# A 256-token, two-model chain of layers on one core: the RWKV time-mixing layer in another order (r and gate projections ahead of v, scores early, one table set for log and exp, bonus by wide matmuls)

## The reference

```python
def rwkv7_time_mix(h, mu, w_r, w_k, w_v, w_o, w0, w1, w2, a0, a1, a2, g1, g2, k_k, k_a, r_k, ln_g, ln_b):
    xx = jnp.pad(h, ((0, 0), (1, 0), (0, 0)))[:, :-1] - h
    xr, xw, xk, xv, xa, xg = [h + xx * mu[i] for i in range(6)]
    r, k, v = xr @ w_r, xk @ w_k, xv @ w_v
    w = -jax.nn.softplus(-(w0 + jnp.tanh(xw @ w1) @ w2)) - 0.5
    a = jax.nn.sigmoid(a0 + (xa @ a1) @ a2)
    g = jax.nn.sigmoid(xg @ g1) @ g2
    kk = heads(k * k_k); kk = kk / norm(kk)          # 16 heads of 64
    k = k * (1 + (a - 1) * k_a)
    decay = jnp.exp(-jnp.exp(heads(w)))
    # per token: S = S*decay + (S @ -kk) (kk*a)^T + v k^T ; y = S @ r
    y = group_norm(y) * ln_g + ln_b
    bonus = jnp.sum(r * k * r_k, -1, keepdims=True) * v
    return ((y + bonus) * g) @ w_o
```

## Time and profile before

| | us |
|---|---|
| median of 3 runs | 2113.77 (2110.63 to 2114.1) |
| the profiled execution's own time | 2107.99 |
| its span, from the first to the last instruction | 2106.2 |
| PE busy in it | 1939.2 |
| of it, the time-mixing layer up to its output projection | about 1115 to 1384 |

### The profile page before, as it was taken

The page is one execution under the profiler, slowest core; times in us unless marked ns, Lnnn a source line. Parts: engine busy times, 40 slices in busy tenths (PEclk is TensorE's granted clock), DMA queues, the critical chain, the costliest instruction groups (busy, mean ns, idle before and its releaser), DMA issues.

```text
span 2106.2 us, 21632 instructions
## 1 busy us (share of the span) xinstructions
PE 1939.2 (92%) x8583; PEld 1426.7 (68%) x8583; DVE 556.3 (26%) x1339; ACT 416.1 (20%) x989; POOL 56.4 (3%) x68
## 2 busy tenths in 40 slices
PE   6999899787689999999998889989999899999998
PEld 4777678666546777677776677847777667737774
DVE  1000202453311000200005853430000343623344
ACT  1000200132111000200006720340000234312431
POOL 0200000000000000000000303000000000000000
PEclk9999999755589999999999985699999999999999
DMA  5745534200033444445453230023545675366630
GB/s 201 246 151 178 124 120 120 100 1 1 0 98 122 137 162 148 133 138 173 127 168 96 95 106 21 1 80 102 178 132 144 112 115 97 74 105 82 101 101 20
DMA packets 190869, 232.21 MB, mean 110 GB/s; under 512 B 22868, under 2 KB 172696, under 8 KB 190792
## 3 DMA queue, kind: packets, MB, share of 16 engines
q1 hardware_dynamic: 188032, 223.85, 38.9%
q0 software_dynamic: 1840, 5.12, 0.8%
q10 hardware_dynamic: 920, 2.16, 0.3%
HBM read 230.07 MB, written 1.05 MB: 110 GB/s over the span
## 4 chain that ended last, share of the span: by engine, by line
PE 63%; DVE 4%; PEld 2%; issue 2%; ACT 2%; POOL 0%; PEldq 0%; DVEq 0%
PE ps L501 22%; PE ps L274 14%; PE ps L519 10%; PE ps L458 5%; PEld ps L274 2%; PE ps L1548 1%; PE ps L1399 1%; PE ps L542 1%; PE ps L2022 1%; PE ps L2038 1%; PE ps L2026 1%; PE ps L1565 1%; PE ps L357 1%; PE ps L2052 1%; PE ps L2057 1%
## 5 line engine op out<-in xcount | busy, mean ns | idle before, releaser
L501 PE MATMUL ps<-hT,ring 128*128 128x256 f32 x2816 | 624.0, 380 | 0.7 <-issue 0.7
L501 PEld LDWEIGHTS ps<-hT,ring 128*128 128x128 f32 x2816 | 536.8, 191 | 108.3 <-issue 39.3
L274 PE MATMUL ps<-hT,ring 128*128 128x272 f32 (+3 forms) x1408 | 334.6, 392 | 5.5 <-issue 3.0
L274 PEld LDWEIGHTS ps<-hT,ring 128*128 128x128 f32 (+2 forms) x1408 | 256.0, 185 | 67.0 <-issue 11.7
L519 PE MATMUL ps<-ring,arena 128*128 128x512 f32 x640 | 287.7, 592 | 0.0
L573 DVE TENSOR_TENSOR arena<-arena,ps 128x256 f32<-128x256 f32 x88 | 37.1, 421 | 850.5 <-ACT arena L558 850.5
L519 PEld LDWEIGHTS ps<-ring,arena 128*128 128x128 f32 x640 | 121.6, 190 | 118.9 <-issue 114.8
L558 ACT ACTIVATE arena<-ps 128x256 f32<-128x256 f32 x88 | 33.8, 384 | 845.0 <-PE ps L501 845.0
L274 PE MATMUL ps<-arena 128*128 128x64 f32 (+6 forms) x384 | 104.3, 439 | 16.5 <-DVE arena L1261 12.7
L458 PE MATMUL ps<-ring,arena 128*128 128x512 f32 (+1 forms) x256 | 112.6, 596 | 1.5 <-ACT arena L2087 0.8
L274 PEld LDWEIGHTS ps<-arena 128*128 128x128 f32 (+2 forms) x384 | 83.9, 309 | 33.0 <-DVE arena L1261 14.8
(11 more groups left out here) (355 smaller groups left out, 1645.6 us busy)
## 6 DMA issues: line engine op xcount, KB each, us to landing
ring<-in_ffn_w_gate SPq DMA_DIRECT2D x44, 1024.0 KB, 5.3
ring<-in_ffn_w_up SPq DMA_DIRECT2D x44, 1024.0 KB, 5.4
ring<-in_ffn_w_down SPq DMA_DIRECT2D x44, 1024.0 KB, 5.0
ring<-in_w_in SPq DMA_DIRECT2D x32, 1024.0 KB, 10.7
ring<-in_ab_w_in SPq DMA_DIRECT2D x13, 1024.0 KB, 5.4
ring<-in_w_out SPq DMA_DIRECT2D x8, 1024.0 KB, 5.0
ring<-in_ab_w_out SPq DMA_DIRECT2D x6, 1024.0 KB, 5.1
ring<-in_c_w_k SPq DMA_DIRECT2D x4, 1024.0 KB, 5.6
```

The costliest lines, as they stand in the source:

```text
L274: last = nc.tensor.matmul(o, l, r, start=(i == 0), stop=(i == len(pairs) - 1))
L501: m = nc.tensor.matmul(ps[:, 4 + j % 2, 256 * w:256 * (w + 1)], slot8(s0 + 3 * q + w)[:, k, c * P:(c + 1) * P], hT[:, k, META:], start=(k ...
```

## The change

All of it is in the time-mixing layer and in the order of its weights.

1. TensorE's list: r blocks 0 and 1 go ahead of `sig`; `pair_scores(0)` comes after r 3, (1) after r 5, (2) and (3) after g1, which now comes before v. The last score bank goes to VectorE, which copies its diagonal blocks and, after the solve, the rest of it.
2. The bonus is 8 matmuls of 256 columns with 16-column weights (`rsel`), a copy to SBUF by VectorE (`bsum`) and two small transposes, all between `tok` and m32.
3. m32 waits for the first two copies of VectorE's t64 scatter alone; the scatter of `tts` is waited for behind m32 and the first g2 piece. Two g2 pieces stand behind t64 instead of one before it.
4. ScalarE loads the table set that has both Ln and Exp by name, and the Tanh/Sigmoid set once; `key_root(7)` comes before Tanh. It makes 1 + (a - 1)*k_a (Identity with scale and bias) where VectorE had a tensor_scalar. The copy of g1's output comes before `decays(7)`, its Sigmoid before v's evictions.
5. VectorE scans into a buffer of its own (`csum`), so that `mid` is no step of the chain, and has one instruction less per block.

The diff, cut to its core:

```diff
+            r_part = square("c_w_r")
+            plan.append(r_part[0])
                          ((64, P), 0, (1, D), d["c_a2"][0].rearrange("p (o n) -> p o n", o=1))])
-            plan += square("c_w_r") + square("c_w_v")
+            plan += r_part[1:]
             plan.append([(P, 0, (KD, 160), d["c_g1"][0].rearrange("(k p) n -> p k n", p=P))])
+            plan += square("c_w_v")
...
-                n = [turn_a("x", p2, 0), turn_a("x", p2, 1)]
+                o = [bank_a(turn_a("x", p2, 0)), bank_d(turn_d("x", p2, 1)) if p2 == 3 else bank_a(turn_a("x", p2, 1))]
...
-                                m.then_inc(to_act, 1)
+                                m.then_inc(to_dve if p2 == 3 and hh == 1 else to_act, 1)
...
             norm_product(KD - 1)
+            pe.wait_ge(mix_ready, 4 * KD)
...
+            def r_product(j):
+                w = r_slot[j // 2]
...
+                n = turn_a("r", j)
+                m = group(bank_a(n)[:, 0:S], [(slot8(w)[:, c, (j % 2) * P:(j % 2 + 1) * P], MB[3][:, c, :]) for c in range(KD)])
+                m.then_inc(to_act, 1)
...
+            r_product(0)
+            r_product(1)
+            s += 1
             take_slot(pe, s)
...
                     nc.tensor.matmul(bank_a(n[i])[:, 0:S], ring[64 * i:64 * i + 64, s % NSLOT, j * P:(j + 1) * P],
                                      low[64 * i:64 * i + 64, :], start=True, stop=True).then_inc(to_act, 1)
             pe.drain().then_inc(slot_used, 1)
+            s += 4
+            r_product(2)
+            r_product(3)
+            pair_scores(0)
+            r_product(4)
+            r_product(5)
+            pair_scores(1)
+            r_product(6)
+            r_product(7)
+            take_slot(pe, s)
+            pe.wait_ge(mix_ready, 6 * KD)
+            g1 = ring[:, s % NSLOT, 0:KD * 160].rearrange("p (k n) -> p k n", k=KD)
+            n = turn_a("g1")
+            group(bank_a(n)[:, 0:S], [(g1[:, c, 0:P], MB[5][:, c, :]) for c in range(KD)])
+            group(bank_a(n)[0:32, S:2 * S], [(g1[:, c, P:160], MB[5][:, c, :]) for c in range(KD)]).then_inc(to_act, 1)
+            pe.drain().then_inc(slot_used, 1)
+            pe.drain().then_inc(mix_used, 1)
             s += 1
-            pe.wait_ge(mix_ready, 4 * KD)
-            for j in range(KD):
-                if j % 2 == 0:
-                    take_slot(pe, s)
-                n = turn_a("r", j)
-                group(bank_a(n)[:, 0:S], [(slot8(s)[:, c, (j % 2) * P:(j % 2 + 1) * P], MB[3][:, c, :]) for c in range(KD)])\
-                    .then_inc(to_act, 1)
-                if j % 2 == 1:
-                    pe.drain().then_inc(slot_used, 1)
-                    s += 1
-                if j >= 4:
-                    pair_scores(j - 4)
-            pe.wait_ge(mix_ready, 5 * KD)
+            pair_scores(2)
+            pair_scores(3)
...
-            n = turn_d("bonus")
-            for t in range(T):
-                for k in range(KD):
-                    m = group(bank_d(n)[:, t * 16 + 2 * k:t * 16 + 2 * k + 2], [(w_rk[:, k, t * P:(t + 1) * P], rsel[:, k, :])])
-            m.then_inc(to_dve, 1)
-            take_slot(pe, s)
-            pe.wait_ge(mix_ready, 6 * KD)
-            g1 = ring[:, s % NSLOT, 0:KD * 160].rearrange("p (k n) -> p k n", k=KD)
-            n = turn_a("g1")
-            group(bank_a(n)[:, 0:S], [(g1[:, c, 0:P], MB[5][:, c, :]) for c in range(KD)])
-            group(bank_a(n)[0:32, S:2 * S], [(g1[:, c, P:160], MB[5][:, c, :]) for c in range(KD)]).then_inc(to_act, 1)
-            pe.drain().then_inc(slot_used, 1)
-            pe.drain().then_inc(mix_used, 1)
-            s += 1
+            n = turn_d("bonus", 0)
+            group(bank_d(n)[64:80, 0:S], [(rsel[:, 16 * k:16 * k + 16], w_rk[:, k, :]) for k in range(KD)]).then_inc(to_dve, 1)
...
-                pe.wait_ge(act_out, job["g1",])
+                pe.wait_ge(act_out, job["v", 0])
...
-            pe.wait_ge(sc_dve, 2)
-            pe.wait_ge(sc_act, 1)
+            pe.wait_ge(dve_out, job["bonus", 0])
+            n = turn_d("bonus", 1)
+            for t in range(T):
+                m = nc.tensor.transpose(bank_d(n)[:, 16 * t:16 * t + 16], bsum[:, t * P:(t + 1) * P], ident[64:80, 64:80])
+            m.then_inc(to_dve, 1)
+            pe.wait_ge(sc_dve, 1)
...
             g2_product(0, 0)
+            pe.wait_ge(sc_dve, 2)
+            pe.wait_ge(sc_act, 1)
...
-            g2_product(1, 0)
...
+            g2_product(1, 0)
             g2_product(1, 1)
...
+                for hh in range(1 if p2 == 3 else 2):
+                    diag, left, corner = score_parts(next_a(), p2, hh)
...
+            nc.scalar.preload_act_table_set(LN_EXP)
...
-            nc.scalar.activation(low[0:64, :], b[0:64, 0:S], ACT.Tanh)
-            nc.scalar.activation(low[64:P, :], b[64:P, 0:S], ACT.Copy).then_inc(act_out, 1)
-            for j in range(KD):
-                nc.scalar.activation(w_ep[:, j, :], next_a()[:, 0:S], ACT.Sigmoid, bias=colB[:, 48 + j:49 + j]).then_inc(act_out, 1)
-                nc.scalar.activation(w_a[:, j, :], next_a()[:, 0:S], ACT.Sigmoid, bias=colB[:, 56 + j:57 + j]).then_inc(act_out, 1)
+            nc.scalar.activation(low[64:P, :], b[64:P, 0:S], ACT.Copy)
             key_root(7)
-            for j in range(KD):
+            nc.scalar.preload_act_table_set("sigmoid_and_others")
+            nc.scalar.activation(low[0:64, :], b[0:64, 0:S], ACT.Tanh).then_inc(act_out, 1)
+            def r_out(j):
+                nc.scalar.activation(w_r[:, j, :], next_a()[:, 0:S], ACT.Copy).then_inc(act_out, 1)
...
-                nc.scalar.activation(w_r[:, j, :], next_a()[:, 0:S], ACT.Copy).then_inc(act_out, 1)
-                if j >= 4:
-                    scores_out(j - 4)
...
+            r_out(0)
+            r_out(1)
+            act.wait_ge(kfix_in, 1)
+            for j in range(KD):
+                nc.scalar.activation(w_ep[:, j, :], next_a()[:, 0:S], ACT.Sigmoid, bias=colB[:, 48 + j:49 + j]).then_inc(act_out, 1)
+                alink(act, nc.scalar.activation(w_a[:, j, :], next_a()[:, 0:S], ACT.Sigmoid, bias=colB[:, 56 + j:57 + j]))
+                nc.scalar.activation(MB[2][:, j, :], w_a[:, j, :], ACT.Identity, scale=colB[:, 72 + j:73 + j],
+                                     bias=kfix[:, j:j + 1]).then_inc(act_out, 1)
+            nc.scalar.preload_act_table_set(LN_EXP)
+            decays(0)
+            r_out(2)
+            decays(1)
+            r_out(3)
+            decays(2)
+            scores_out(0)
+            r_out(4)
+            decays(3)
+            r_out(5)
+            decays(4)
+            scores_out(1)
+            r_out(6)
+            decays(5)
+            r_out(7)
+            decays(6)
+            b = next_a()
+            nc.scalar.activation(sg1, b[:, 0:S], ACT.Copy)
+            nc.scalar.activation(sg2, b[0:32, S:2 * S], ACT.Copy).then_inc(act_out, 1)
+            decays(7)
+            scores_out(2)
+            scores_out(3)
             alink(act, nc.scalar.activation(emid, mid[:, :, 1], ACT.Exp, scale=-DECAY))
             nc.scalar.activation(eend, w_c[:, :, P - 1], ACT.Copy).then_inc(emid_done, 1)
+            alink(act, nc.scalar.activation(sg1, sg1, ACT.Sigmoid))
+            alink(act, nc.scalar.activation(sg2, sg2, ACT.Sigmoid))
...
-            b = next_a()
+            nc.scalar.preload_act_table_set(LN_EXP)
             act.wait_ge(solved, 1)
-            nc.scalar.activation(sg1, b[:, 0:S], ACT.Sigmoid)
-            nc.scalar.activation(sg2, b[0:32, S:2 * S], ACT.Sigmoid).then_inc(act_out, 1)
-            act.wait_ge(tt_zero, 3)
+            act.wait_ge(tt_zero, 2)
...
-            for k in range(KD):
-                nc.vector.tensor_scalar(rsel[:, k, :], const("pairsel"), col(80, k), None, ALU.mult)
+            nc.vector.tensor_scalar(kfix, colB[:, 72:80], -1.0, 1.0, ALU.mult, ALU.add).then_inc(kfix_in, 1)
...
+            dve.wait_ge(mix_ready, 6 * KD)
+            dlink(dve, nc.vector.memset(rsel, 0.0))
+            for a in range(2):
+                nc.vector.tensor_scalar(rsel[:, a:a + 127 - 1 + 1:18], colB[:, 80:88], const("pairsel")[:, a:a + 1], None, ALU.mult)
...
-                        m = nc.vector.tensor_tensor_scan(w_c[:, j, tk], ones, w_ep[:, j, tk], 0.0, ALU.mult, ALU.add)
+                        m = nc.vector.tensor_tensor_scan(csum[:, t, :], ones, w_ep[:, j, tk], 0.0, ALU.mult, ALU.add)
                     dlink(dve, m)
                     c2 = w_c[:, j, :].rearrange("p (t n) -> p t n", t=T)
-                    dlink(dve, nc.vector.tensor_copy(mid[:, j, :], c2[:, :, 63]))
-                    dlink(dve, nc.vector.tensor_tensor(c2, c2, mid[:, j, :].rearrange("p (t o) -> p t o", o=1).broadcast_to([P, T, P]),
-                                                       ALU.subtract))
+                    dlink(dve, nc.vector.tensor_tensor(c2, csum, csum[:, :, 63:64].broadcast_to([P, T, P]), ALU.subtract))
+                    nc.vector.tensor_copy(mid[:, j, :], csum[:, :, 63])
```

(23 more changed lines are left out.)

44 lines of the change are left out of this document (29 added, 15 removed).

## The result

The changed kernel takes 2080.24 us (median of 4 runs, 2079.41 to 2081.34) against 2112.54 for the kernel before: a ratio of 0.9848, 95% interval 0.9834 to 0.9863, or 32 us less. Forecast were 2099.8, with a range of 2086 to 2110. The sign was right and the time outside the range: the gain is more than twice the forecast's.

The account below looks back on a forecast made before the run. Three limits in turn: VectorE's per-block chain, the chain from solve to m32, then TensorE at half clock. -12.1 and -2.8, with 1 back for the clock, gave -14: 2099.8 us from a 2113.77 median, range 2086 to 2110.

Parts of the forecast that it names:

- The start of the chain: Start of VectorE's per-block chain: `sig` 2.6 us later, 1.25 us a block on ScalarE, first block ready 2.4 us later.
- TensorE between `sig` and the solve: TensorE has more to do than the wait allows, with `decays(7)` behind g1's evictions; the solve starts 2.8 us later.
- From the solve to m32: After the solve, v, `tok`, wide bonus (3.5 us) and VectorE's copies let m32 start at 1250.0, 12.1 us earlier.
- m32 to the end of chunk t = 0: Same matmuls in another order, 37.50 and 50.07 us at clock 0.50; no change taken.
- Chunk t = 1: Group norm in the last chunk: fewer table loads, so roots are waited for less, 2.8 us saved (1.3 to 4.4).
- The clock stays at 1.00 through m32 to chunk t = 0: Rival: TensorE keeps full clock from m32 through chunk t = 0, another 28 us off, 2072 us; chance 0.10.
- The slower rival: Rival: the clock is not back in time, chunk t = 1 takes 50.07 us instead of 34.24; 2118.6 us, chance 0.05.
- The gain is eaten before the solve: Rival: clock falls and queued evictions between first scores and solve start the solve 10 us later; 2110 us, chance 0.07.

Follow-up runs that it names:

- e15_k_on_vector: e13_high_last with the key's factor computed on VectorE again and without ScalarE's Identity: 2077.10 us.
- e14_bonus_narrow: e13_high_last with the wide bonus undone: 128 matmuls of 2 columns again, no copy and no transposes of the sum: 2077.23 us.
- e5_delay_17: The changed kernel with one extra matmul of 432 columns in front of g2(1,1), to hold TensorE up by 1.7 us: 2106.31 us.
- e3_tables_own: The changed kernel without the four lines that name a table set, so the compiler picks the sets (34 loads in the layer): 2107.96 us.
- e13_high_last: The changed kernel with the last g2 matmuls reordered, the two over 32 rows ahead of the two over 128 rows: 2096.89 us.
- e12_version2: e4 with ScalarE's `tts[1]` scatter earlier, g2's 32-row halves spread and all four 128-row halves ahead of chunk t = 0: four runs 2065.46 to 2072.91 us, one 2095.18.
- e1_g2_apart: The changed kernel with g2(1,0) put back between the m64 and t64 products: 2080.07 us.
- e9: e3_tables_own with the last two g2 pieces reordered, both 32-row matmuls first, then both 128-row ones: 2081.66 us.
- e17: e13_high_last with one extra matmul of 256 columns ahead of its last g2 pieces, to hold TensorE up by 1.0 us: 2081.00 us.
- e2: The kernel before with only g2(1,0) moved from between m64 and t64 to right ahead of g2(1,1): 2095.99 us.
- e6: The kernel before with extra matmuls of 512 and 80 columns in front of g2(1,1), to hold TensorE up by 2.3 us: 2090.22 us.
- e4: The changed kernel with the wide bonus ahead of `tok`, t64 copies ahead of the bonus sum's, m32 ahead of the bonus transposes: 2077.25 us.
- e7: e3_tables_own with one extra matmul of 256 columns in front of g2(1,1), to hold TensorE up by 1.0 us: 2083.51 us.
- e8: The kernel before with only the change's table sets named: five runs at 2082.86 to 2091.22 us, five at 2107.28 to 2109.78.

## Why the prediction was wrong

*The start of the chain, +2.4; measured +4.05.* `sig` was right (+2.5 for +2.6). The block was not: from the first block's first Sigmoid to the second's it is 1.38 us (1174.52 to 1175.90), for the 1.25 taken, and all eight take 11.25 for 10.0. The mis-sized term is the Identity: 0.60 us long, and 0.51 from its start to the next Sigmoid's, for 0.40. e15_k_on_vector takes it away and gets 3.4 us back in that stage, but only 2.0 at m32.

*TensorE between `sig` and the solve, +2.8; measured +3.4.* The mechanism stands as it was given: `decays(7)` behind g1's eviction, VectorE waiting 2.62 us. The clock did fall to 0.50 there, as the range allowed for, from 1178.3 to 1188.5, and the next two r blocks took 9.1 us for 7.2; TensorE still waited 0.98 us for VectorE behind them, so that it cost nothing at the scores.

*From the solve to m32, -12.1; measured -11.3.* Right in size, and one of its parts was not weighed: the bonus was costed for TensorE (3.5, measured 3.6), while the wait it puts on VectorE was taken as given. e14_bonus_narrow shows that the old form would have been 2.3 us better there.

*m32 to the end of chunk t = 0, "I take no change".* The first half of it was right, -0.6. The second half is the step that failed: chunk t = 0 itself, put at no change and measured at -20.7 us. The forecast had read from the earlier trace rows that a busy TensorE may stay at 0.50, which holds. (It did not stay there from 1244 on, as the forecast has it: the clock was at 1.00 again from 1250.9 to 1257.7 and fell in the wait ahead of m32.) It then took the clock of one execution as a property of the code. The runs show instead that this stretch has two outcomes some 20 us apart, and that a microsecond of shift picks one; the order of the four matmuls ahead of the chunk bears on it too, as far as single profiles tell. The extra matmul meant for 1.7 us made the changed kernel 26 us slower, that of 2.3 us made the kernel before 22 faster, and that of 1.0 us the one with its own table loads 24 faster; in the layer alone it is +22.9, -21.0 and -20.7. Both outcomes hold steadily where nothing near by shifts: all 57 runs of the kernel before lie at 2107.85 us or above, all four of the changed kernel at 2081.34 or below. That is why one profile looks like a rule.

*Chunk t = 1, -2.8; measured -4.6.* The forecast took the clock's rise at 1349.73 for the chunk's start, which came at 1348.02. So it missed that the chunk began at 0.50. e5_delay_17 has the changed kernel's table loads and a chunk t = 1 that also begins with some 2 us at 0.50; it takes 32.1 us. So 3.9 of the 4.6 are the loads (35.95 to 32.1), within the forecast's 1.3 to 4.4, and 0.7 the clock (32.1 to 31.3). What was missed is that the loads also cost 2.9 ahead of chunk t = 0 (e3_tables_own).

*The rivals.* "The clock stays at 1.00 through m32 to chunk t = 0", 2072 us at a chance of 0.10, was nearest in time and not what happened: m32 to t64 ran at 0.50, and the clock came back in chunk t = 0. By the section of the Trainium skill it was drawn from ("TensorE: Matmul & The Clock Gate", "Why this matters for your kernels") 37 busy microseconds should not have been at 0.50. No trace here agrees with that: in each of the 19 the clock falls at least 24 us ahead of chunk t = 0 and is back at the earliest 2.6 us ahead of it. The slower rival's outcome was real: e13_high_last and one run of e12_version2 have chunk t = 1 at 0.50, after a second fall. "The gain is eaten before the solve" did not happen; the solve was 3.4 later, not 10. What the list lacked is the clock back in one chunk alone. With it as a case of even chance the forecast would have had two times, 2099.8 and 2099.8 - 20.7 = 2079, and a range holding both. That 2079 would have come so near to the measured 2080.24 is in part luck: the layer gained 37.1 us, and some 5 were lost outside it.

The same page of the Trainium skill, "TensorE: Matmul & The Clock Gate", says in its section "What's actually happening" that the monitor behind the clock runs freely, so that the point of change depends on where the matmuls land in its rhythm. The runs are in line with that; what they add is that not only the point of the change can hang on where the matmuls land, but whether there is one for the next 48 us.

**What stays open.** How much of the 20.7 us the pair of g2 pieces deserves: it was not needed (e1_g2_apart), and it did not suffice (e3_tables_own, e5_delay_17). With the 128-row halves last the clock came back in all nine kernels built so (e9 to e17), between 2.6 us ahead of the chunk and 1.6 us into it; that this holds from every start is not shown, nor why the seam to chunk t = 1 then took the clock away in e13 and once in e12.

Not followed up is what the change costs outside the layer. In the profiles of the 7 kernels with the compiler's own table loads the layer starts at 1116 to 1125 us, 1120 on average; in those of the 12 that name their sets it starts at 1121 to 1128, 1126 on average. The wait at 104 us is 2.3 us or less in the 7, and 3.1 to 4.4 in the 12; in it TensorE stands behind SyncE's issue of a weight DMA, which took 0.45 us before and 3.99 after. Naming the sets is what the 12 have in common and the 7 lack; why it should slow an early issue is open. Behind the start of w_o there is one more pair of outcomes: 721 to 723 us in 15 profiles and 727 to 728 in four (e2, e3, e5, e12), with 18 to 24 us of it at 0.50 in the one case and 35 in the other. Differences of medians above hold these parts too, which is why they exceed those of the layer.

## What to carry over

Take a stage's start from its first matmul and not from the place where the clock changes. Where the granted clock in a profile changes only near a seam, treat the stretch on either side as having two possible times and give both; ahead of a verdict on a change of a few microseconds, compare the granted clock by stage, since a gain or a loss of 1% can be the clock's and not the edit's. A dummy matmul of 1 to 2 us ahead of such a seam is a cheap test for it. And cost a widened product also for the engine that must wait for it before it may do its own urgent copies.

## What the runs showed of the hardware

A table load took 1283 ns wherever it stood, and the compiler placed one for each change between log and exp: 16 for 8 pairs of them, 8 on each of two lines in the earlier trace rows's view, although one set holds both.

With TensorE busy in nearly all of it, the clock stayed at 0.50 from m32 into the first 1.7 us of chunk t = 1 in the kernel before (87.6 us) and for 43.3 us in e13_high_last, while in other kernels it rose within 4 us of the chunk's start. In the last 3.4 us ahead of the rise in e6, and in the last 5.7 in e9, stood 128-row and 64-row matmuls alone. Where 32-row and 128-row halves of g2 came in turn, fully busy, it rose in five profiles (the changed kernel, e1, e2, e4, e7) and did not in four (before, e3, e5, e8). An ACTIVATE Identity that reads a bias and a scale column took 0.60 us on 128x256 where a Copy took 0.38 and a Sigmoid 0.47.
